# Delta rule's output norm: sums and squares of the next group issued a group ahead, and two of four diagonal matrices built on ScalarE

## The chip, the cores and the metric

The kernel runs on one core of one Trainium2 chip. The metric is the device time of one execution in microseconds, as the median of several runs. The engines named below are TensorE (PE; its weight loads are PEld), VectorE (DVE), ScalarE (ACT), GpSimd (POOL) and SyncE (SP), which issues the loads of weights. Each engine works through its own instructions in the order written and waits on semaphores where the code says so.

## The reference, cut to what matters

The reference is a network of two blocks on 256 tokens of width 1024. The change lies in one step of its second block, the bidirectional gated delta rule with 8 heads of 128 columns. What follows the two scans is:

```
o = jnp.transpose(o_fwd + o_bwd, (0, 2, 1, 3))                          # (B, S, H, 128)
o = o * lax.rsqrt(jnp.mean(o * o, axis=-1, keepdims=True) + RMS_EPS)    # per token and head
o = o * norm_w.astype(f32) * jax.nn.silu(z.astype(f32))
return o.reshape(B, S, H * DV).astype(h.dtype) @ w_out
```

So each row (one token of one head) is divided by its root mean square, multiplied by a gate, and the result goes through the output projection.

## The kernel before

The kernel is hand-written: every engine has a list of instructions fixed by the code, with no scheduler, and counts on semaphores between them. The step around the change is the end of `gdn_solve`. The 8 heads are worked in four groups `q` of two heads; a group has four 128x128 pieces `c` (two heads by two tiles of tokens).

For one group the work passes from engine to engine:

1. PE, `read_out(q)`: 8 pairs of products (16 matmul instructions of 128x128 in the trace, L2535 and L2537) into bank `ps[4 + q]`, then `o_mm`.
2. DVE, L2823: adds `from_state` to that bank, which gives `o` of the group, 128x512, then `o_out`.
3. ACT, L2702: four Square instructions over 128x128, each with a sum over its row into `o_sum` (an activation and a read of the accumulator in the trace), each with `o_square`.
4. DVE, L2825 and L2827: mean plus epsilon, reciprocal, 128x4 each, then `o_means`.
5. ACT, L2705: square root of the four columns into `o_root`, then `o_roots`.
6. DVE, L2835: four diagonal matrices `diag`, identity times a column of `o_root`, then `diag_ready`.
7. PE, L2546, `turn(q)`: four products `o` x `diag` (8 matmul instructions in the trace), which transpose and scale in one, into `ps[q]`, then `o_turned`.
8. DVE, L2809, `gate(q)`; ACT, L2697, `round_out(q)`; DVE, L2816, `split_out(q)`: gate, high part, low part, 128x512 each.

PE's list is `read_out(0)`, `read_out(1)`, `turn(0)`, `read_out(2)`, `turn(1)`, `read_out(3)`, `turn(2)`, the first part of the output projection (8 matmuls, L2558, over the heads of groups 0 and 1), `turn(3)`, and the rest of the output projection. PE's list is the same before and after the change: `read_out(q + 2)` stands behind `turn(q)`.

In the list of DVE, `gate(q - 1)` and `split_out(q - 2)` stand between the reciprocal and the diagonals of group `q`; in ACT's, `round_out(q - 1)` stands behind the root of group `q`. The weights of the output projection are in the ring of four buffers before the step begins, and SP issues nothing during it.

Of the kernel before, what the change touches and what calls it, by code (L numbers as in the profile page):

```python
# [20 lines left out]
ACT = mybir.ActivationFunctionType  # L21
AX = mybir.AxisListType

P = 128
# [153 lines left out]
def carve(k, at, *dims):  # L178

    n = int(np.prod(dims))  # L180
    assert at + n <= k.ARENA, (at, n)
    v = k.arena[:, at:at + n]
    if len(dims) == 1:
        return v
    names = "abcd"[:len(dims)]
    return v.rearrange(f"p ({' '.join(names)}) -> p {' '.join(names)}",
                       **{x: d for x, d in zip(names[1:], dims[1:])})
# [1296 lines left out]
GROUPS = S // GROUP_T  # L1484
# [830 lines left out]
def gdn_solve(k, seam):  # L2315


    g, ps, U, H = k.gdn, k.ps, FIRST, GDN_H
# [10 lines left out]
    lay = Layout(k, g.at_A)  # L2329
    v1, state = lay.take(2 * H, P), lay.take(2 * H, P)  # L2330
    rhs, v2 = g.kq.rearrange("p h (d n) -> p (h d) n", d=2), carve(k, g.at_v, 2 * H, P)
    lay = Layout(k, g.at_kdec + 2 * H * S)
    o, junk, diag = lay.take(2 * H, P), lay.take(4, P), lay.take(2, 4, P)
    gated, from_state = carve(k, g.at_kdec, H, S), carve(k, g.at_kdec, 2 * H, P)
    oT = [k.spare_r[:, n * H * S:(n + 1) * H * S].rearrange("p (h s) -> p h s", h=H) for n in range(2)]
    o_sum, o_mean, o_inv, o_root = (k.small[:, n * 16:(n + 1) * 16] for n in range(4))
# [13 lines left out]
    GROUPS = H // 2  # L2350
# [11 lines left out]
    def group(ap, q):  # L2362
        return ap[:, 4 * q:4 * q + 4, :].rearrange("p c n -> p (c n)")
# [5 lines left out]
    def tensor(pe):  # L2369
# [41 lines left out]
        for h in range(H):  # L2411
            for tt in range(TT):
                c = slice(tt * P, (tt + 1) * P)
                at = (h % 2) * S + tt * P
                last = pe.matmul(ps[h // 2][:, at:at + P], g.kT[:, h, c], g.qT[:, h, c], start=True, stop=True)
# [97 lines left out]
        for q in range(GROUPS):  # L2513


            for c in range(4):
                h, tt = 2 * q + c // 2, c % 2
                last = pe.matmul(ps[4 + q][:, c * P:(c + 1) * P], g.qT[:, h, tt * P:(tt + 1) * P],
                                 state[:, 2 * h + 1 - tt, :], start=True, stop=True)
# [21 lines left out]
        def turn(q):  # L2541


            pe.wait_ge(diag_ready, q + 1)
            for c in range(4):
                last = pe.matmul(ps[q][:, c * P:(c + 1) * P], o[:, 4 * q + c, :], diag[:, q % 2, c, :],  # L2546
                                 start=True, stop=True)
            last.then_inc(o_turned, 1)
# [3 lines left out]
        def out_of(n, tt, parts, heads):  # L2552

            hi, lo = unit_parts(k, U["gdn_out"] + n)
            for m in parts:
                split_ready(k, pe, U["gdn_out"] + n, m)
                for h in heads:
                    last = pe.matmul(out_bank(n, tt), oT[m == 1][:, h, tt * P:(tt + 1) * P], (hi, hi, lo)[m][:, h, :],  # L2558
                                     start=(m == 0 and h == 0), stop=(m == 2 and h == H - 1))
            return last  # L2560

        for q in range(GROUPS):
            read_out(q)
            if q >= 1:
                turn(q - 1)
        pe.wait_ge(o_out, 2)
        pe.wait_ge(o_round, 2)
        for tt in range(TT):
            out_of(0, tt, (0,), range(4))
        turn(3)  # L2570
        pe.wait_ge(o_out, 4)
        pe.wait_ge(o_round, 4)
# [3 lines left out]
        for tt in range(TT):  # L2576
            last = out_of(0, tt, (1, 2), range(H))
        last.then_inc(k.unit_done, 1)
        for n in range(1, 4):
            for tt in range(TT):  # L2580
                last = out_of(n, tt, (0, 1, 2), range(H))
# [4 lines left out]
    def scalar(act):  # L2586
        for h in range(H):
# [6 lines left out]
            for s in range(4):  # L2594
                last = act.activation(g.intraT[:, h, s, :], RI[h % 2][:, s * P:(s + 1) * P], ACT.Exp,
                                      bias=g.negG[:, s, h:h + 1])
# [87 lines left out]
        for q in range(GROUPS):  # L2684
            act.wait_ge(qs_mm, q + 1)
            for c in range(4):
                h, tt = 2 * q + c // 2, c % 2
                last = act.activation(from_state[:, 4 * q + c, :], ps[4 + q][:, c * P:(c + 1) * P], ACT.Copy,
                                      scale=g.eG[:, 2 - tt, h:h + 1])
# [3 lines left out]
        def round_out(q):  # L2693

            act.wait_ge(o_gated, q + 1)
            heads = slice(2 * q, 2 * q + 2)
            act.activation(oT[0][:, heads, :], gated[:, heads, :], ACT.Copy).then_inc(o_round, 1)  # L2697

        for q in range(GROUPS):
            act.wait_ge(o_out, q + 1)  # L2700
            for c in range(4):
                act.activation(junk[:, c, :], o[:, 4 * q + c, :], ACT.Square,  # L2702
                               accum_out=o_sum[:, 4 * q + c:4 * q + c + 1]).then_inc(o_square, 1)
            act.wait_ge(o_means, q + 1)
            act.activation(o_root[:, 4 * q:4 * q + 4], o_inv[:, 4 * q:4 * q + 4], ACT.Sqrt).then_inc(o_roots, 1)  # L2705
            if q >= 1:
                round_out(q - 1)
        round_out(3)
# [7 lines left out]
    def vector(dve):  # L2716
        dve.wait_ge(g.evacuated, H + H // 2)
        for h in range(H):
            dve.wait_ge(keys_mm, h + 1)
            dve.wait_ge(decays_ready, h + 1)  # L2720
            for s in range(4):
                decay = g.dA[:, h % 2, s, :] if s < 2 else g.intraT[:, h, s, :]
                c = slice(s % 2 * P, (s % 2 + 1) * P)
                last = dve.scalar_tensor_tensor(out=g.A[:, h, s, :], in0=decay, scalar=g.beta[:, s, h:h + 1],
                                                in1=KK[h % 2][:, c], op0=ALU.mult, op1=ALU.mult)
# [60 lines left out]
        for h in range(H):  # L2786
            dve.wait_ge(kq_out, h // 2 + 1)
            at = g.intraT[:, h].rearrange("p (d t) n -> p d (t n)", d=2)
# [3 lines left out]
        for q in range(GROUPS):  # L2792

            dve.wait_ge(ks_mm, q + 1)
            for c, (h, d) in enumerate(members[q]):
                s = second_s[d]
                last = dve.scalar_tensor_tensor(out=rhs[:, 2 * h + d, :], in0=ps[q][:, c * P:(c + 1) * P],
                                                scalar=g.nbe[:, s, h:h + 1], in1=g.bv[:, h, s, :],
                                                op0=ALU.mult, op1=ALU.add)
# [5 lines left out]
        def gate(q):  # L2805

            dve.wait_ge(o_turned, q + 1)
            heads = slice(2 * q, 2 * q + 2)
            dve.scalar_tensor_tensor(out=flat(gated[:, heads, :]), in0=ps[q][:, :], scalar=col(k, "gdn_norm"),  # L2809
                                     in1=flat(g.zT[:, heads, :]), op0=ALU.mult, op1=ALU.mult).then_inc(o_gated, 1)  # L2810

        def split_out(q):

            dve.wait_ge(o_round, q + 1)
            heads = slice(2 * q, 2 * q + 2)
            dve.tensor_tensor(oT[1][:, heads, :], gated[:, heads, :], plain(oT[0][:, heads, :]), ALU.subtract)\  # L2816
               .then_inc(o_split, 1)

        for q in range(GROUPS):
            at = slice(4 * q, 4 * q + 4)  # L2820
            dve.wait_ge(o_mm, q + 1)
            dve.wait_ge(qs_out, q + 1)
            dve.tensor_tensor(group(o, q), ps[4 + q][:, :], group(from_state, q), ALU.add).then_inc(o_out, 1)  # L2823
            dve.wait_ge(o_square, 4 * (q + 1))
            own.up(dve.tensor_scalar(o_mean[:, at], o_sum[:, at], 1.0 / P, EPS, ALU.mult, ALU.add))  # L2825
            own.settle(dve)
            dve.reciprocal(o_inv[:, at], o_mean[:, at]).then_inc(o_means, 1)  # L2827
            if q >= 1:
                gate(q - 1)
            if q >= 2:  # L2830
                split_out(q - 2)
            dve.wait_ge(o_out, q + 1)
            dve.wait_ge(o_roots, q + 1)
            for c in range(4):
                last = dve.tensor_scalar(diag[:, q % 2, c, :], k.ident, o_root[:, 4 * q + c:4 * q + c + 1], None,  # L2835
                                         ALU.mult)
                if c < 3:
                    own.up(last)
            last.then_inc(diag_ready, 1)
# [3 lines left out]
        for n in range(4):  # L2843
            dve.wait_ge(k.unit_done, U["gdn_out"] + n + 1)
            for tt in range(TT):
                xs = k.x[:, tt, n * S:(n + 1) * S]
                last = dve.tensor_tensor(xs, xs, ps[(4 + 2 * n + tt) % 8][:, 0:S], ALU.add)
# [5 lines left out]
            if n == 2:  # L2853
                split_lo(k, dve, U["mlp1_0"])
                seam.round_lo(dve, 1)
                seam.round_lo(dve, 2)

    return Stage(gpsimd=gpsimd, tensor=tensor, scalar=scalar, vector=vector)


# [569 lines left out]
def back_half(k, before_experts):  # L3430
# [7 lines left out]
    gdn_layout(k)  # L3438
    project = gdn_project(k, after_experts)
    rule = gdn_solve(k, after_rule)  # L3440
    feed = mlp(k, 0, after_rule, after_feed)
    dilated = ds_layer(k, after_feed, after_dilated)
# [218 lines left out]
```

## Time and profile before

| what | value |
|---|---|
| median of 3 runs | 1942.78 us (1939.44 to 1943.89) |
| profiled execution | 1942.14 us |
| its span | 1940.3 us |
| granted TensorE clock, mean of the span | 0.984 |
| PE busy | 1870.4 us, 96% of the span |
| PEld busy | 1731.5 us, 89% |
| DVE busy | 1293.1 us, 67% |
| ACT busy | 907.9 us, 47% |
| the step of the change, start of the first sum to start of the rest of the projection | 1358.83 to 1378.59 us |

The profiled execution's time is 1.84 us longer than its span, and 0.64 us below the median. Times inside the span are counted from its start. A timeline row gives the start, the time from the start of the first to the end of the last instruction of the row, the engine, the line, what is written from what, and, in brackets, how long the engine stood idle before it and for whom.

### The profile page before, as it was taken

The numbers are of one execution on the slowest core, as the hardware profiler recorded it, in microseconds if no ns is written. First come the engines' busy times: TensorE is split into PE (matmuls) and PEld (weight loads), VectorE is DVE, ScalarE is ACT, GpSimd is POOL, SyncE is SP. The second block draws the span as 40 slices with busy tenths as digits, with TensorE's granted clock in tenths as the row PEclk, the third lists the DMA queues.
The fourth block names the chain that finished last, engine by engine and source line by source line (L and its number), as shares of the span: only waits on it lengthen the run. The fifth ranks groups of instructions, "written<-read, shape, count | busy, mean of one in ns | idle before, by whom it ended". The sixth has DMA issues, their size and how long they took to land. (4 is left out here: it accounts for less than half of the span.)

```text
span 1940.3 us, 31388 instructions
## 1 busy us (share of the span) xinstructions
PE 1870.4 (96%) x13055; PEld 1731.5 (89%) x13055; DVE 1293.1 (67%) x2048; ACT 907.9 (47%) x1206; POOL 18.0 (1%) x24
## 2 busy tenths in 40 slices
PE   7999899999999999999999989978899999999998
PEld 7998898899999999988888879878899889889987
DVE  5667773899788888755555567996566455546654
ACT  6457543343334443444444445775355343445533
POOL 0000000000000000000000000000000001000000
PEclk9999899999999999999999999997999999999999
DMA  6444355354444444465555553320254456625443
GB/s 228 174 159 152 109 177 192 131 176 175 151 151 153 153 153 141 164 227 192 190 191 190 191 197 108 137 83 23 79 182 173 175 214 197 144 70 202 176 171 151
DMA packets 44757, 310.66 MB, mean 160 GB/s; under 512 B 5182, under 2 KB 5694, under 8 KB 8160
## 3 DMA queue, kind: packets, MB, share of 16 engines
q1 hardware_dynamic: 42592, 303.58, 43.4%
q0 software_dynamic: 1472, 4.86, 1.6%
q8 instruction: 87, 1.43, 0.3%
q10 hardware_dynamic: 576, 0.55, 0.1%
q14 instruction: 30, 0.25, 0.0%
HBM read 306.84 MB, written 2.13 MB: 159 GB/s over the span
## 5 line engine op out<-in xcount | busy, mean ns | idle before, releaser
L310 DVE TENSOR_TENSOR s_ring_lo<-s_ring,s_w_hi 128x2048 fp32r<-128x2048 f32 x236 | 540.5, 2291 | 220.9 <-ACT s_w_hi L304 216.3
L304 ACT ACTIVATE s_w_hi<-s_ring 128x2048 fp32r<-128x2048 f32 x235 | 448.4, 1908 | 124.4 <-PE bank L347 53.4
L347 PE MATMUL bank<-s_hT_hi,s_ring_lo 128*128 128x256 f32 x2000 | 282.3, 284 | 8.9 <-DVE s_ring_lo L310 8.7
L347 PE MATMUL bank<-s_hT_hi,s_w_hi 128*128 128x256 f32 x2000 | 288.6, 287 | 2.2 <-ACT s_w_hi L304 1.9
L347 PEld LDWEIGHTS bank<-s_hT_hi,s_ring_lo 128*128 128x128 f32 x2000 | 259.0, 193 | 9.9 <-DVE s_ring_lo L310 9.9
L347 PEld LDWEIGHTS bank<-s_hT_hi,s_w_hi 128*128 128x128 f32 x2000 | 259.1, 193 | 7.0 <-issue 5.6
L1650 PE MATMUL bank<-s_w_hi,s_hT_lo 128*128 128x512 f32 x1008 | 238.8, 389 | 0.3 <-issue 0.3
L1650 PEld LDWEIGHTS bank<-s_w_hi,s_hT_lo 128*128 128x128 f32 x1008 | 189.1, 188 | 39.7 <-issue 0.4
L347 PE MATMUL bank<-s_hT_lo,s_w_hi 128*128 128x256 f32 x1040 | 147.7, 285 | 0.0
L347 PEld LDWEIGHTS bank<-s_hT_lo,s_w_hi 128*128 128x128 f32 x1040 | 136.0, 195 | 0.0
L347 PE MATMUL bank<-s_x_r,s_w_hi 128*128 128x256 f32 x960 | 134.8, 283 | 0.0
L2903 DVE TENSOR_TENSOR s_ring_lo<-s_ring,s_spare_r 128x2048 fp32r<-128x2048 f32 x32 | 73.2, 2291 | 81.6 <-ACT s_spare_r L2889 81.6
L1752 ACT ACTIVATE s_hT_lo<-s_arena 128x512 fp32r (+1 forms) x64 | 40.4, 632 | 184.6 <-PE bank L1650 184.6
L1650 PE MATMUL bank<-s_ring_lo,s_hT_lo 128*128 128x512 f32 x504 | 124.5, 389 | 0.0
L347 PEld LDWEIGHTS bank<-s_x_r,s_w_hi 128*128 128x128 f32 x960 | 123.8, 192 | 0.0
L2930 PE MATMUL bank<-s_spare_r,s_mid_r 128*128 128x512 f32 x512 | 119.5, 389 | 0.0
L2930 PEld LDWEIGHTS bank<-s_spare_r,s_mid_r 128*128 128x128 f32 x512 | 95.9, 188 | 19.8
L1650 PEld LDWEIGHTS bank<-s_ring_lo,s_hT_lo 128*128 128x128 f32 x504 | 94.6, 188 | 19.6
L1929 DVE TENSOR_TENSOR s_hT_lo<-s_arena,s_hT_lo 128x512 fp32r<-128x512 f32 x64 | 44.3, 692 | 90.8 <-ACT s_hT_lo L1752 90.8
L2889 ACT ACTIVATE s_spare_r<-s_ring 128x2048 fp32r<-128x2048 f32 x32 | 61.3, 1917 | 89.4 <-DMA s_ring<-weights 89.3
L1726 ACT ACTIVATE s_arena<-bank 128x344 f32<-128x344 f32 (+31 forms) x64 | 20.5, 320 | 173.7 <-DVE s_arena L1902 173.7
L272 PE MATMUL bank<-s_hT,s_ring 128*128 128x256 f32 x384 | 84.3, 379 | 0.9 <-ACT s_hT L463 0.9
(452 smaller groups left out, 2444.4 us busy)
## 6 DMA issues: line engine op xcount, KB each, us to landing
s_ring<-weights SPq DMA_DIRECT2D x282, 1024.0 KB, 4.8
s_arena<-bias_by_distance POOLq DMA_DIRECT2D x12, 384.0 KB, 7.3
s_arena<-mem SPq DMA_DIRECT2D x1, 1024.0 KB, 6.0
s_x<-x SPq DMA_DIRECT2D x1, 1024.0 KB, 13.9
x_away<-s_x SPq DMA_DIRECT2D x1, 1024.0 KB, 6.3
s_arena<-sub_keys SPq DMA_DIRECT2D x1, 1024.0 KB, 8.4
s_arena<-x_away SPq DMA_DIRECT2D x1, 1024.0 KB, 7.0
out<-s_x SPq DMA_DIRECT2D x2, 512.0 KB, 2.6
```

The costliest lines, as they stand in the source:

```text
L272: last = pe.matmul(out[:, nb * S:(nb + 1) * S], w[:, c, nb * P:(nb + 1) * P], srcT[:, c, :], start=(c == 0), stop=(c == 7))
L304: act.activation(k.w_hi[:, u % 2, :], k.ring[:, u % RING, :], ACT.Copy).then_inc(k.hi_ready, 1)
L310: dve.tensor_tensor(k.ring_lo[:, u % RING, :], k.ring[:, u % RING, :], plain(k.w_hi[:, u % 2, :]), ALU.subtract).then_inc(k.lo_ready, 1)
L347: last = pe.matmul(out[:, nb * S:(nb + 1) * S], w[:, c, nb * P:(nb + 1) * P], h[:, c, :], start=(n == 0 and c == 0), stop=(n == 2 and c == 7))
L1650: last = pe.matmul(ps[4 + 2 * tt + dh][:, :], g[:, b, tt * P:(tt + 1) * P], w[:, b, dh * 512:(dh + 1) * 512], start=(d == 0 and n == 0 and ...
L1726: act.activation(slots_of(k.G, g * GROUP_T)[:, c:, :], bank[g][:, :].rearrange("p (t n) -> p n t", t=GROUP_T)[:, c:, :], ACT.Copy)\
L1752: round_up = lambda d, at: act.activation(weighted_hi[:, d % 2], k.G[:, at, :], ACT.Copy)\
L1929: take = lambda d, at: dve.tensor_tensor(weighted_lo[:, d % 2], k.G[:, at, :], plain(weighted_hi[:, d % 2]), ALU.subtract).then_inc(weight ...
L2889: act.activation(wide_hi[:, u % RING], slot(k, u), ACT.Copy).then_inc(k.hi_ready, 1)
L2903: dve.tensor_tensor(lo, w, plain(wide_hi[:, u % RING]), ALU.subtract).then_inc(k.lo_ready, 1)
L2930: last = pe.matmul(ps[4 + 2 * pair + tt][:, :], m[:, 8 * q + c, tt * P:(tt + 1) * P], w[:, c, at, :], start=(q == 0 and n == 0 and c == 0) ...
```

## The change

Three things change, in ACT's and DVE's lists alone. The add of group `q + 1` is put ahead of the mean of group `q` on DVE. The four squares of group `q + 1` are put ahead of the root of group `q` on ACT (their scratch output has eight pieces where it had four). Of the four diagonals of a group, ACT makes the first two, behind a wait for its own root, and DVE the last two; PE waits for both counts. The diff, whole:

```diff
--- before.py
+++ after.py
@@ -2330,7 +2330,7 @@
     v1, state = lay.take(2 * H, P), lay.take(2 * H, P)
     rhs, v2 = g.kq.rearrange("p h (d n) -> p (h d) n", d=2), carve(k, g.at_v, 2 * H, P)
     lay = Layout(k, g.at_kdec + 2 * H * S)
-    o, junk, diag = lay.take(2 * H, P), lay.take(4, P), lay.take(2, 4, P)
+    o, junk, diag = lay.take(2 * H, P), lay.take(8, P), lay.take(2, 4, P)
     gated, from_state = carve(k, g.at_kdec, H, S), carve(k, g.at_kdec, 2 * H, P)
     oT = [k.spare_r[:, n * H * S:(n + 1) * H * S].rearrange("p (h s) -> p h s", h=H) for n in range(2)]
     o_sum, o_mean, o_inv, o_root = (k.small[:, n * 16:(n + 1) * 16] for n in range(4))
@@ -2541,7 +2541,7 @@
         def turn(q):
 
 
-            pe.wait_ge(diag_ready, q + 1)
+            pe.wait_ge(diag_ready, 2 * (q + 1))
             for c in range(4):
                 last = pe.matmul(ps[q][:, c * P:(c + 1) * P], o[:, 4 * q + c, :], diag[:, q % 2, c, :],
                                  start=True, stop=True)
@@ -2696,13 +2696,24 @@
             heads = slice(2 * q, 2 * q + 2)
             act.activation(oT[0][:, heads, :], gated[:, heads, :], ACT.Copy).then_inc(o_round, 1)
 
-        for q in range(GROUPS):
+        def o_squares(q):
+
             act.wait_ge(o_out, q + 1)
             for c in range(4):
-                act.activation(junk[:, c, :], o[:, 4 * q + c, :], ACT.Square,
+                act.activation(junk[:, 4 * (q % 2) + c, :], o[:, 4 * q + c, :], ACT.Square,
                                accum_out=o_sum[:, 4 * q + c:4 * q + c + 1]).then_inc(o_square, 1)
+
+        o_squares(0)
+        for q in range(GROUPS):
+            if q + 1 < GROUPS:
+                o_squares(q + 1)
             act.wait_ge(o_means, q + 1)
             act.activation(o_root[:, 4 * q:4 * q + 4], o_inv[:, 4 * q:4 * q + 4], ACT.Sqrt).then_inc(o_roots, 1)
+            act.wait_ge(o_roots, q + 1)
+            for c in range(2):
+                last = act.activation(diag[:, q % 2, c, :], k.ident, ACT.Copy,
+                                      scale=o_root[:, 4 * q + c:4 * q + c + 1])
+            last.then_inc(diag_ready, 1)
             if q >= 1:
                 round_out(q - 1)
         round_out(3)
@@ -2816,11 +2827,17 @@
             dve.tensor_tensor(oT[1][:, heads, :], gated[:, heads, :], plain(oT[0][:, heads, :]), ALU.subtract)\
                .then_inc(o_split, 1)
 
-        for q in range(GROUPS):
-            at = slice(4 * q, 4 * q + 4)
+        def add_state(q):
+
             dve.wait_ge(o_mm, q + 1)
             dve.wait_ge(qs_out, q + 1)
             dve.tensor_tensor(group(o, q), ps[4 + q][:, :], group(from_state, q), ALU.add).then_inc(o_out, 1)
+
+        add_state(0)
+        for q in range(GROUPS):
+            at = slice(4 * q, 4 * q + 4)
+            if q + 1 < GROUPS:
+                add_state(q + 1)
             dve.wait_ge(o_square, 4 * (q + 1))
             own.up(dve.tensor_scalar(o_mean[:, at], o_sum[:, at], 1.0 / P, EPS, ALU.mult, ALU.add))
             own.settle(dve)
@@ -2831,7 +2848,7 @@
                 split_out(q - 2)
             dve.wait_ge(o_out, q + 1)
             dve.wait_ge(o_roots, q + 1)
-            for c in range(4):
+            for c in range(2, 4):
                 last = dve.tensor_scalar(diag[:, q % 2, c, :], k.ident, o_root[:, 4 * q + c:4 * q + c + 1], None,
                                          ALU.mult)
                 if c < 3:
```

ACT, from the last copy of `v2` (L2675 in both) to the first rounding, before the change:

```order
L2675 ACTIVATE s_arena<-bank,s_gdn_small 128x128 x2
L2702 ACTIVATE s_arena,s_small<-s_arena 128x128 x4
L2705 ACTIVATE s_small<-s_small 128x4
L2702 ACTIVATE s_arena,s_small<-s_arena 128x128 x4
L2705 ACTIVATE s_small<-s_small 128x4
L2697 ACTIVATE s_spare_r<-s_arena 128x512
```

and after it, where L2703 are the squares, L2711 the root, L2714 the two diagonals and L2697 the rounding:

```order
L2675 ACTIVATE s_arena<-bank,s_gdn_small 128x128 x2
L2703 ACTIVATE s_arena,s_small<-s_arena 128x128 x8
L2711 ACTIVATE s_small<-s_small 128x4
L2714 ACTIVATE s_arena<-s_consts,s_small 128x128 x2
L2703 ACTIVATE s_arena,s_small<-s_arena 128x128 x4
L2711 ACTIVATE s_small<-s_small 128x4
L2714 ACTIVATE s_arena<-s_consts,s_small 128x128 x2
L2697 ACTIVATE s_spare_r<-s_arena 128x512
```

Eight squares, those of groups 0 and 1, now stand ahead of the root of group 0, and the squares of group 2 ahead of the root of group 1.

DVE, from the first add, groups 0 and 1, before the change:

```order
L2823 TENSOR_TENSOR s_arena<-bank,s_arena 128x512
L2825 TENSOR_SCALAR s_small<-s_small 128x4
L2827 RECIPROCAL s_small<-s_small 128x4
L2835 TENSOR_SCALAR s_arena<-s_consts,s_small 128x128 x4
L2823 TENSOR_TENSOR s_arena<-bank,s_arena 128x512
L2825 TENSOR_SCALAR s_small<-s_small 128x4
L2827 RECIPROCAL s_small<-s_small 128x4
L2809 SCALAR_TENSOR_TENSOR s_arena<-bank,s_cols,s_arena 128x512
L2835 TENSOR_SCALAR s_arena<-s_consts,s_small 128x128 x4
```

and after it, where L2834 is the add, L2842 and L2844 mean and reciprocal, L2852 the diagonals and L2820 the gate:

```order
L2834 TENSOR_TENSOR s_arena<-bank,s_arena 128x512 x2
L2842 TENSOR_SCALAR s_small<-s_small 128x4
L2844 RECIPROCAL s_small<-s_small 128x4
L2852 TENSOR_SCALAR s_arena<-s_consts,s_small 128x128 x2
L2834 TENSOR_TENSOR s_arena<-bank,s_arena 128x512
L2842 TENSOR_SCALAR s_small<-s_small 128x4
L2844 RECIPROCAL s_small<-s_small 128x4
L2820 SCALAR_TENSOR_TENSOR s_arena<-bank,s_cols,s_arena 128x512
L2852 TENSOR_SCALAR s_arena<-s_consts,s_small 128x128 x2
```

Two adds, of groups 0 and 1, now stand ahead of the first mean, and two diagonals stand where four stood.

## Rows read from the trace of the kernel before

**Rows 1.** The page, engines: busy us, share of the span, instructions

```profile
PE 1870.4 (96%) x13055; PEld 1731.5 (89%) x13055; DVE 1293.1 (67%) x2048; ACT 907.9 (47%) x1206; POOL 18.0 (1%) x24
```

**Rows 2.** Busy time by stretch: us, engines in turn, clock, DMA share, GB/s

```profile
1358.00:1380.00 22.00, 14.06 (x102) 13.02 (x101) 12.26 (x36) 8.65 (x41) 0.00 (x0) 0.88 0.00 1
...
1400.00:1500.00 100.00, 99.85 (x818) 98.96 (x817) 64.43 (x61) 52.98 (x63) 0.00 (x0) 1.00 0.52 183
```

**Rows 3.** Timeline of PE, through the step

```profile
1356.84 0.39 PE L2535 MATMUL bank<-s_arena 128*128 128x128 f32 x2
...
1360.19 0.39 PE L2537 MATMUL bank<-s_arena 128*128 128x128 f32 x2
1362.53 1.16 PE L2546 MATMUL bank<-s_arena 128*128 128x128 f32 x8 [1.95 <-DVE s_arena L2835]
1363.52 0.39 PE L2535 MATMUL bank<-s_arena 128*128 128x128 f32 x2
...
1365.08 0.39 PE L2537 MATMUL bank<-s_arena 128*128 128x128 f32 x2
1366.27 1.16 PE L2546 MATMUL bank<-s_arena 128*128 128x128 f32 x8 [0.80 <-DVE s_arena L2835]
...
1370.62 1.16 PE L2546 MATMUL bank<-s_arena 128*128 128x128 f32 x8 [1.40 <-DVE s_arena L2835]
...
1374.96 2.08 PE L2546 MATMUL bank<-s_arena 128*128 128x128 f32 x8 [2.24 <-DVE s_arena L2835]
1378.59 3.46 PE L2558 MATMUL bank<-s_w_hi,s_spare_r 128*128 128x256 f32 x16 [1.55 <-issue]
...
1384.76 2.08 PE L2558 MATMUL bank<-s_w_hi,s_spare_r 128*128 128x256 f32 x16
```

**Rows 4.** Timeline of DVE, group 0 and parts of the later ones

```profile
1358.83 0.69 DVE L2823 TENSOR_TENSOR s_arena<-bank,s_arena 128x512 f32<-128x512 f32 x1 [5.19 <-PE bank L2537]
1360.87 0.17 DVE L2825 TENSOR_SCALAR s_small<-s_small 128x4 f32<-128x4 f32 x1 [1.34 <-ACT s_arena L2702]
1361.07 0.18 DVE L2827 RECIPROCAL s_small<-s_small 128x4 f32<-128x4 f32 x1
1361.60 0.87 DVE L2835 TENSOR_SCALAR s_arena<-s_consts,s_small 128x128 f32<-128x128 f32 x4 [0.34 <-ACT s_small L2705]
1362.38 0.68 DVE L2823 TENSOR_TENSOR s_arena<-bank,s_arena 128x512 f32<-128x512 f32 x1
...
1368.46 0.72 DVE L2809 SCALAR_TENSOR_TENSOR s_arena<-bank,s_cols,s_arena 128x512 f32<-128x512 f32 x1
1369.10 0.68 DVE L2816 TENSOR_TENSOR s_spare_r<-s_arena,s_spare_r 128x512 fp32r<-128x512 f32 x1
1369.69 0.87 DVE L2835 TENSOR_SCALAR s_arena<-s_consts,s_small 128x128 f32<-128x128 f32 x4
...
1377.08 0.75 DVE L2809 SCALAR_TENSOR_TENSOR s_arena<-bank,s_cols,s_arena 128x512 f32<-128x512 f32 x1 [2.17 <-PE bank L2546]
```

**Rows 5.** Timeline of ACT in the step

```profile
1359.56 0.31 ACT L2702 ACTIVATE s_arena<-s_arena 128x128 f32<-128x128 f32 x1 [1.36 <-DVE s_arena L2823]
1359.77 0.19 ACT L2702 ACTIVATION_READ_ACCUMULATOR s_arena<-s_arena 128x1 f32 x1
...
1361.29 0.20 ACT L2705 ACTIVATE s_small<-s_small 128x4 f32<-128x4 f32 x1 [0.45 <-DVE s_small L2827]
...
1377.86 0.63 ACT L2697 ACTIVATE s_spare_r<-s_arena 128x512 fp32r<-128x512 f32 x1 [3.67 <-DVE s_arena L2809]
```

**Rows 6.** The same timeline earlier: sixteen scaled 128x128 copies out of PSUM

```profile
1350.79 4.24 ACT L2688 ACTIVATE s_arena<-bank,s_gdn_small 128x128 f32<-128x128 f32 x16 [2.36 <-PE bank L2518]
```

**Rows 7.** PE by stretch: us, busy (instructions), granted clock, DMA share, GB/s

```profile
1370.60:1374.90 4.30, 2.11 (x16) 0.98 0.00 0
1374.90:1378.50 3.60, 2.08 (x8) 0.50 0.00 0
1378.50:1381.50 3.00, 2.91 (x13) 0.50 0.00 0
```

## The prediction

> **What bounds the kernel now.** I read the page first: PE is busy 96% of the span, DVE 67%, ACT 47% [rows 1]. Then the busy time by stretch: around the change it looks different. In 1358 to 1380 us PE is busy 14.06 of 22 us, DVE 12.26, ACT 8.65, with no DMA at work; in 1400 to 1500 us PE is busy 99.85 of 100 [rows 2]. So this step is bound by a chain between engines, nothing is loaded in it, and PE is full behind it: what the step loses or gains goes into the time one for one. Last, the timelines of the three engines, to follow the chain. PE's four `turn`s start at 1362.53, 1366.27, 1370.62 and 1374.96 us, each after an idle time that DVE's diagonals end, and the rest of the projection starts at 1378.59 [rows 3]. The intervals are 3.74, 4.35, 4.34 and 3.63 us.
>
> What a group takes, from group 0: the add starts at 1358.83, the squares at 1359.56 (0.73 later), the mean at 1360.87 (1.31), the root at 1361.29 (0.42), the diagonals at 1361.60 (0.31), `turn` at 1362.53 (0.93) [rows 3 to 5]. The next add starts at 1362.38, right behind the diagonals, though PE had ended `read_out(1)` at 1360.19 + 0.39 = 1360.58. That wait looks like something to save. The point of this prediction is what the look-ahead hangs on instead.
>
> **The change, step by step.** The squares of group q + 1 now stand ahead of the root of group q. They need the add of q + 1, which needs `read_out(q + 1)`. On PE, `read_out(q + 2)` stands behind `turn(q)`. So the new chain is: `turn(q)`, `read_out(q + 2)`, add, four squares, and only then the root of q + 1, its diagonals and `turn(q + 1)`. Before, `read_out(q + 2)` had the whole of DVE's and ACT's work on group q + 1 to hide behind; now it is on the path. Behind ACT's waiting square stand the root, the two diagonals and the rounding; for the root wait DVE's diagonals and PE.
>
> Root to `turn`. Before it is 1362.53 - 1361.29 = 1.24 us. Now DVE makes two diagonals: 0.31 to its first, 0.20 between two (four take 0.87 and one takes 0.28: (0.87 - 0.28) / 3), 0.28 for the last, 0.05 to PE: 0.84. ACT's half: no row shows ACT waiting for its own result. Nearest are the root's 0.20 us and DVE's reciprocal, which starts 0.20 after the mean that it needs [rows 4, 5]; 0.20 to 0.31 bounds it. A scaled copy from SBUF isn't shown either: a square of that size takes 0.31 and lets the next start after 0.21 [rows 5], and sixteen scaled copies out of PSUM take 4.24, 0.265 each [rows 6]. So 0.20 to 0.31, plus 0.21 to 0.265, plus 0.31, plus 0.05: 0.77 to 0.94. I take 0.84 for both halves, as DVE's and the middle of ACT's agree: 0.4 us saved a group, the bounds of ACT's half adding up to 0.1 each. The Trainium skill ("VectorE: DVE Perf Modes", section on the TRN2 errata) says that ScalarE pays a fixed extra on each SBUF-source instruction, exposed between instructions. This trace agrees in the duration of one (0.31 us for a square), but not in the spacing, since the next starts after 0.21 [rows 5]; by the page two copies would take 0.1 us more than by the row, in each of four groups.
>
> Group 0. `read_out(1)` ends at 1360.58, the add of group 1 starts at 1360.60, its squares 0.73 later at 1361.33. They hold ACT for 1.19 us (the 1.31 above less the signal and the 0.10 by which the next instruction starts before the last one has ended), so the root of group 0 starts at 1362.52, where it started at 1361.29. The mean and reciprocal (0.42) are hidden in that. `turn(0)` starts at 1362.52 + 0.84 = 1363.36: 0.83 later than before.
>
> Groups 1 and 2. From `turn(q)`: 0.99 to the start of `read_out(q + 2)` (1362.53 to 1363.52), 1.95 to its end (1365.08 + 0.39) [rows 3], 0.02 to the add, 0.73 to the squares, 1.19 to the root, 0.84 to the next `turn`: 5.72 us. DVE's work of the interval fits: add 0.59 to the next, mean 0.20, reciprocal 0.10, gate 0.64, split 0.59 [rows 4], 2.12 us against the 2.23 from the add to its diagonals. `turn(1)` starts at 1369.08 and `turn(2)` at 1374.80, which were 1366.27 and 1370.62.
>
> Group 3. No more look-ahead, and mean and reciprocal are early. But the gate of group 2 stands ahead of the diagonals of group 3 on DVE and waits for `turn(2)`: 1.16 for it, 0.04 to the gate, 0.64 gate, 0.59 split [rows 3, 4], 0.20 + 0.28 + 0.05 for the diagonals: 2.96 where it was 4.34. `turn(3)` starts at 1377.76, was 1374.96.
>
> The rest, `turn(3)` to the projection, stays: 2.08 and 0.04, the gate 0.78, the rounding 0.73 [rows 3 to 5]. In all +2.8 us (0.83 + 1.98 + 1.37 - 1.38), with TensorE's clock as it is now.
>
> **The clock.** In 1370.6 to 1374.9 PE was busy 2.11 of 4.30 us, and the granted clock fell to 0.50, that is 1.2 in place of 2.4 GHz, through `turn(3)` and to 1381.5 [rows 7]. `turn(3)` took 2.08 where the others took 1.16, and 16 matmuls of the projection 3.46 where such a row at full clock takes 2.08 [rows 3]: before already pays 0.92 + 1.38 = 2.3 us. After the change PE is idle 5.72 - 2.94 = 2.8 us before each `turn`, more than the 2.24 us of idle time around which it fell. `turn` and `read_out` at the lower level are 2.94 x 2.08 / 1.16 = 5.3 us: 2.3 more for each such interval. Nothing at all extra, or even the 2.3 given back if the clock happens to be full at the end, is the one bound: +2.8 - 2.3 = +0.5. Both intervals and `turn(2)` low is the other: 2.8 + 4.6 + 0.9 = +8.3. I take one interval low: the idle time is longer than where it fell, but between there are 2.9 busy us. The Trainium skill ("TensorE: Matmul & The Clock Gate", what's actually happening) says that the clock follows how busy PE has been recently; the fall in the rows agrees, and by this rule the change, which lengthens PE's idle times, tends to lose more than its chain does.
>
> **The sum.** Against the profiled execution, 1942.14 us (1940.3 of span and 1.84 around it; 0.64 below the median): 1942.14 + 2.8 + 2.3 = 1947.2 us. That is 4.4 us or 0.23% above the median. I count 0.2%, 3.9 us, as about what a measurement of this kernel can tell from no change.
>
> **The rivals.**
> - *The chain alone.* The clock falls no more than before, or gives something back: +0.5 to +3.8, around 1944.9, which can't be told from no change. For it speaks that `turn` and `read_out` fill half of each interval; against it that the clock fell with 2.11 of 4.30 us busy. 0.30.
> - *The clock low in most of the step:* +6.5 to +8.3, around 1949.4. For it: three idle times of 2.8 us in a row. Against it: with the clock low PE is busy for more of the time, and at 1381.5 it came back after 2.91 busy us of 3.00 [rows 7]. 0.13.
> - *The look-ahead works, faster.* If the add and squares of group q + 1 were done when the root of q is due, squares and sum would be off the path, and intervals would shrink to PE's own 2.94 us: (3.74 + 4.35 + 4.34) - 3 x 2.94 = 3.6, plus 0.4 in group 0, so 1938.1. It is decided by whether `read_out(q + 1)` ends 1.9 us (0.73 + 1.19) before the root of q is due. In group 0 it ends at 1360.58 and the root is due at 1361.29, 0.7 us: too late by 1.2; later it stands behind the `turn` of the group before last. Only if ACT could take its root ahead of a waiting square could this be; its rows stand in the order written. The Trainium skill ("TensorE: Matmul & The Clock Gate", architectural detail) calls ScalarE's queue strictly first in, first out, with which these rows agree. 0.04.
> - *The change cancels out:* the 0.4 saved in each group meets a look-ahead less late than worked out, within 1.5 us of zero, 1942 to 1943. 0.05.
>
> The likeliest case, the chain and about one interval's clock (+3.8 to +6.5, 1945.9 to 1948.6), has 0.48. Of it about 0.09 lies below the bound. So slower by over 0.2%: 0.39 + 0.13 = 0.52; within: 0.30 + 0.09 + 0.05 = 0.44; faster: 0.04. For 8 in 10 the range takes in most of the chain alone (from +1.9) and of the low clock (to +7.9): 1944.0 to 1950.0.
>
> **What would show it.** In the changed kernel's timeline: the first root 1.2 us later after the first add than before (3.7 in place of 2.46); `turn` intervals of 5.7, 5.7 and 3.0; ACT's squares idle for DVE's add ahead of each root; two diagonals on each engine, `turn` 0.84 behind the root; PE's idle time 2.8 ahead of `turn(0)` to `turn(2)`; the granted clock below 1.00 somewhere in 1361 to 1378. Wrong would be: intervals under 4.4 us (the chain isn't through `read_out`), a clock at full all through the step (the chain alone), or a last `turn` less than 2 us later than before.

## The result, and the profile after

The changed kernel takes 1947.89 us (median of 14 runs, 1943.17 to 1949.78), where the kernel before takes 1941.49 us (median of 14, 1938.84 to 1944.9). The ratio is 1.003, with a 95% interval of 1.0022 to 1.0037: slower by 0.2 to 0.4%, beyond the 0.2% that the prediction set. The forecast was 1947.2 us, with a range of 1944.0 to 1950.0.

The profiled execution has a span of 1945.6 us, 5.3 more than before. PE's timeline through the step, beside [rows 3] (L2546 is `turn`, L2535 and L2537 `read_out`, L2558 the projection):

```profile
1358.59 0.39 PE L2537 MATMUL bank<-s_arena 128*128 128x128 f32 x2
1361.89 1.16 PE L2546 MATMUL bank<-s_arena 128*128 128x128 f32 x8 [2.91 <-ACT s_arena L2714]
1362.89 0.41 PE L2535 MATMUL bank<-s_arena 128*128 128x128 f32 x2
...
1365.66 0.63 PE L2537 MATMUL bank<-s_arena 128*128 128x128 f32 x2
1369.21 1.43 PE L2546 MATMUL bank<-s_arena 128*128 128x128 f32 x8 [2.92 <-ACT s_arena L2714]
...
1376.69 2.03 PE L2546 MATMUL bank<-s_arena 128*128 128x128 f32 x8 [2.91 <-ACT s_arena L2714]
...
1380.56 1.16 PE L2546 MATMUL bank<-s_arena 128*128 128x128 f32 x8 [0.18 <-DVE s_arena L2852]
1383.27 3.47 PE L2558 MATMUL bank<-s_w_hi,s_spare_r 128*128 128x256 f32 x16 [1.55 <-issue]
```

Three times PE stands idle for 2.9 us until ScalarE's diagonals come. The intervals between turns are 7.32, 7.48 and 3.87 us, where they were 3.74, 4.35 and 4.34. A last row of `read_out` (1365.66 here) lasts 0.63, where it took 0.39 at full clock: the clock is low there. DVE's timeline, beside [rows 4] (L2834 is the add, L2852 two diagonals):

```profile
1357.23 0.69 DVE L2834 TENSOR_TENSOR s_arena<-bank,s_arena 128x512 f32<-128x512 f32 x1 [5.19 <-PE bank L2537]
...
1366.33 0.69 DVE L2834 TENSOR_TENSOR s_arena<-bank,s_arena 128x512 f32<-128x512 f32 x1 [4.62 <-PE bank L2537]
...
1373.82 0.69 DVE L2834 TENSOR_TENSOR s_arena<-bank,s_arena 128x512 f32<-128x512 f32 x1 [4.80 <-PE bank L2537]
```

and ACT's, beside [rows 5] (L2703 the squares, L2711 the root, L2714 the two copies that make diagonals):

```profile
1367.05 0.31 ACT L2703 ACTIVATE s_arena<-s_arena 128x128 f32<-128x128 f32 x1 [5.21 <-DVE s_arena L2834]
...
1368.24 0.19 ACT L2711 ACTIVATE s_small<-s_small 128x4 f32<-128x4 f32 x1
1368.46 0.69 ACT L2714 ACTIVATE s_arena<-s_consts,s_small 128x128 f32<-128x128 f32 x2
```

DVE waits 4.6 and 4.8 us for `read_out`, ACT 5.2 us for DVE, and the root of group 1 comes at 1368.24, right behind the squares of group 2. Its mean and reciprocal had been ready before. The clock by stretch (us, PE busy, granted clock, DMA share, GB/s), beside [rows 7]:

```profile
1361.80:1369.20 7.40, 4.40 (x24) 0.77 0.01 2
1369.20:1376.60 7.40, 4.57 (x24) 0.77 0.00 0
1376.60:1380.50 3.90, 3.69 (x16) 0.56 0.00 0
1380.50:1383.20 2.70, 1.16 (x8) 1.00 0.00 0
1383.20:1386.20 3.00, 2.93 (x15) 0.57 0.00 0
```

A granted clock of 0.50 is the lower level (1.2 GHz), 1.00 the full one (2.4 GHz), and a value between them is a mean over time at each: it switches between the two all through the step. I measure a step's length from the first add to the start of the projection. It was 1378.59 - 1358.83 = 19.76 us and is 1383.27 - 1357.23 = 26.04: 6.3 longer. The span grew by less because in this execution all that lies ahead of the first add was 1.6 us shorter, and what lies behind 0.6 longer.

### The profile page after: what moved, and what is told of

It reads as the page before. It is cut to its first block and busy times, and to the rows that moved or that the text cites. A ratio compares the mean times of both kernels' runs of the same rounds, so it can differ in the third digit from the quotient of the medians.

```text
span 1945.6 us, 31388 instructions
## 1 busy us (share of the span) xinstructions
PE 1873.2 (96%) x13055; PEld 1734.3 (89%) x13055; DVE 1292.0 (66%) x2040; ACT 909.5 (47%) x1214; POOL 18.0 (1%) x24
```

## The experiments

The theory: the look-ahead made the root of group q + 1 wait for `read_out(q + 2)`, which stands behind `turn(q)` on PE, so that each `turn` waits for a `read_out` behind the one before it; and PE's longer idle times let its clock fall. The rivals were ScalarE's share of the diagonals as the cause, and the squares' place in ScalarE's list by itself. All ratios are to the kernel before, run beside each of them, with 95% intervals: its median was 1942.48 us beside e1 to e4, 1942.53 beside e5 to e8 and 1943.06 beside e9 and e10, so the ratios tell more than the medians. Step lengths are as above, of one profiled execution each.

| kernel | median us | ratio | step us | turn intervals us |
|---|---|---|---|---|
| before | 1941.49 | 1 | 19.76 | 3.74, 4.35, 4.34 |
| changed | 1947.89 | 1.003 (1.0022 to 1.0037) | 26.04 | 7.32, 7.48, 3.87 |
| e1 diagonals only | 1942.75 | 0.9994 (0.9983 to 1.0005) | 17.27 | 3.22, 3.96, 3.95 |
| e2 look-ahead only | 1950.4 | 1.0045 (1.0032 to 1.0058) | 26.97 | 6.12, 8.66, 3.63 |
| e3 changed, PE's order | 1939.09 | 0.9983 (0.9974 to 0.9992) | 16.23 | 2.78, 3.07, 3.00 |
| e4 before, PE's order | 1942.47 | 1.0002 (0.9993 to 1.0011) | 18.85 | 3.74, 4.35, 4.35 |
| e5 changed, PE kept busy | 1944.29 | 1.0009 (1.0 to 1.0018) | 22.09 | 5.87, 5.85, 3.00 |
| e6 before, PE kept busy | 1940.95 | 0.9992 (0.9983 to 1.0001) | 18.83 | 3.74, 4.34, 4.35 |
| e7 changed, late squares | 1945.85 | 1.0015 (1.0006 to 1.0024) | 22.72 | 5.05, 7.27, 3.91 |
| e8 late squares, PE's order | 1936.79 | 0.997 (0.9958 to 0.9982) | 15.93 | 2.78, 2.98, 3.37 |
| e9 diagonals, PE's order | 1941.3 | 0.9994 (0.9984 to 1.0004) | 17.27 | 3.22, 3.96, 3.95 |
| e10 e8, PE kept busy | 1938.56 | 0.9977 (0.9968 to 0.9986) | 15.25 | 2.79, 2.98, 2.99 |

The instructions ahead of the first add are the same in all twelve kernels, yet their traces reach it between 1354.83 us (e5) and 1360.10 (e2). So from one trace each the steps can be compared, and whole times only to some 5 us. The profiled executions of e5 and e10 are the fastest of their 11 runs, 4.8 and 5.1 us below the medians.

**e1, the diagonals alone** (edit of the kernel before):

```diff
-            pe.wait_ge(diag_ready, q + 1)
+            pe.wait_ge(diag_ready, 2 * (q + 1))
...
             act.activation(o_root[:, 4 * q:4 * q + 4], o_inv[:, 4 * q:4 * q + 4], ACT.Sqrt).then_inc(o_roots, 1)
+            act.wait_ge(o_roots, q + 1)
+            for c in range(2):
+                last = act.activation(diag[:, q % 2, c, :], k.ident, ACT.Copy,
+                                      scale=o_root[:, 4 * q + c:4 * q + c + 1])
+            last.then_inc(diag_ready, 1)
...
-            for c in range(4):
+            for c in range(2, 4):
```

> The kernel before with one part of the change: two of the four diagonals of a group on ScalarE, no look-ahead. The theory (the look-ahead carries the loss, the split of the diagonals is a small gain): root to turn about 1.0 us in place of 1.24 in group 0, intervals between turns 3.3, 4.0 and 4.0 in place of 3.74, 4.35 and 4.34, the time 1 to 4 us below the kernel before (the chain 1.3, the rest if the clock then falls less). The rival (the scaled copies on ScalarE and its wait for its own root are what costs): intervals longer than before, 2 us or more slower.

The intervals came as expected and the step is 2.5 us shorter, so ScalarE's copies don't lose anything in it: 0.3 us up to the first `turn`, 1.3 in the intervals, and 0.9 because `turn(3)` now ran at full clock. Yet the time isn't measurably lower, where 1 to 4 us had been expected. In its profiled execution what lies behind the step, from the start of the projection to the end of the span, is 1941.0 - 1374.59 = 566.4 us, against 1940.3 - 1378.59 = 561.7 before. Where that went, in stretches of e1 (us, PE busy, clock, DMA share, GB/s):

```profile
1374.50:1381.50 7.00, 6.91 (x36) 0.58 0.00 0
...
1640.00:1648.00 8.00, 8.00 (x40) 0.59 0.57 105
```

and of the same places before:

```profile
1378.50:1385.50 7.00, 6.91 (x47) 0.78 0.00 0
1638.80:1650.80 12.00, 11.15 (x73) 1.00 0.65 139
```

In the first 7 us of the projection the clock is lower (36 matmuls done in place of 47), and 260 us later, in the dilated attention, it falls where it didn't before. These two, (0.78 - 0.58) x 7 = 1.4 us and (1.00 - 0.59) x 8 = 3.3 us of full clock, are the 4.7 us. That is one execution of e1; its 12 runs lie between 1936.2 and 1946.01, and whether the later fall is in most of them isn't known. It doesn't explain the ratio either: e9 below has the same step length and the same ratio, and its trace is at 1.00 through that piece.

**e2, the look-ahead alone** (the changed kernel, `diag` by DVE for `c in range(4)` again, no copies on ACT, PE waits for `q + 1`).

> The changed kernel with all four diagonals back on VectorE, the look-ahead alone. The theory: the chain turn, read_out, add, squares, root is in it whole, intervals 6.1 us at full clock and up to 7.6 at the low one, the time 5 to 9 us above the kernel before, at least as slow as the changed kernel. The rival (ScalarE's diagonals carry the loss): at the time of the kernel before, within 2 us.

As the theory had it in the main: the step is the longest, 7.2 us over before, and the first interval 6.12. The second, with the clock low, is 8.66, more than the 7.6 expected. The look-ahead carries the whole loss. In the step the split of the diagonals makes up 0.9 us of it; in the time the intervals of the two ratios overlap, so that isn't shown. The rival that ScalarE's diagonals cost is out.

**e3 and e4, PE's order** (the changed kernel, and the kernel before):

```diff
         for q in range(GROUPS):
             read_out(q)
-            if q >= 1:
-                turn(q - 1)
+            if q >= 2:
+                turn(q - 2)
+        turn(2)
```

> The changed kernel with one more edit: TensorE takes read_out(q + 2) ahead of turn(q) in place of behind it. The theory (the look-ahead fails because read_out of its group stands behind a turn that it holds up): squares wait for nothing of PE any more, intervals 2.8 to 3.1 us in place of 7.3, 7.5 and 3.9, the clock not fallen or fallen once, the time 3 to 6 us below the kernel before. The rival (squares ahead of the root are bad for ScalarE's own load, whatever PE does): intervals over 4.4 us, no faster than before.

> The kernel before with TensorE's new order alone (read_out(q + 2) ahead of turn(q)), no look-ahead and all diagonals on VectorE. A control for the run before it: by the theory the turns start when they did, intervals 3.7, 4.35 and 4.35, and the chain gives nothing; the clock may move the time by -2 to +1 us. The rival (TensorE's order is a gain by itself): 3 us or more faster with shorter intervals.

PE's timeline in e3:

```profile
1362.64 1.16 PE L2546 MATMUL bank<-s_arena 128*128 128x128 f32 x8 [1.13 <-ACT s_arena L2715]
1365.42 1.06 PE L2546 MATMUL bank<-s_arena 128*128 128x128 f32 x8
1368.49 1.16 PE L2546 MATMUL bank<-s_arena 128*128 128x128 f32 x8 [2.02 <-ACT s_arena L2715]
```

With the same lists on ACT and DVE as in the changed kernel, and only `read_out` moved ahead, the step falls from 26.04 to 16.23 us and the kernel is 0.17% faster than before, 1.0030 against 0.9983. The same order in the kernel before gives nothing in the time (1.0002) or the intervals between turns. Its step is 0.9 us shorter, by the clock. It was low around `turn(2)` in e4, where PE then had to wait for DVE all the same, and no longer in `turn(3)`, where the projection waits for it:

```profile
1371.08 1.63 PE L2546 MATMUL bank<-s_arena 128*128 128x128 f32 x8 [3.19 <-DVE s_arena L2836]
1375.43 1.16 PE L2546 MATMUL bank<-s_arena 128*128 128x128 f32 x8 [1.01 <-DVE s_arena L2836]
```

So the cause of the longer chain is the pair: a look-ahead, and a producer (`read_out(q + 2)`) that stands on PE behind `turn(q)`. The squares' place alone isn't it.

**e5 and e6, PE kept busy.** Products whose results are overwritten, on PE alone:

```diff
+        def fill(bank, n):
+            for i in range(n):
+                pe.matmul(ps[bank][:, 0:P], g.qT[:, 0, 0:P], g.qT[:, 1, 0:P], start=True, stop=True)
...
             if q >= 1:
+                fill(q - 1, [10, 10, 10][q - 1])
                 turn(q - 1)
```

In e6 the counts are 0, 0 and 4, and `fill(3, 7)` stands ahead of `turn(3)`.

> The changed kernel with work added on TensorE that only keeps it busy: ten products of 128x128 (twenty matmul instructions, about 2.2 us at full clock) ahead of each of turn(0), turn(1) and turn(2), where it stood idle for 2.9 us. Their results are overwritten. The theory (beside the longer chain the clock's fall costs 2 to 3 us): granted clock at 1.00 from the first add to turn(2), intervals near 5.8, 5.8 and 3.0 in place of 7.3, 7.5 and 3.9, the time 2 to 5 us below the changed kernel, so 0 to 4 us above the kernel before. The rival (the clock's level doesn't matter here, the chain alone is longer than was worked out): time within 1 us of the changed kernel or above it.

> The kernel before with such busy work: four products ahead of turn(2) and seven ahead of turn(3), inside its idle times of 1.4 and 2.2 us. The theory: intervals unchanged at 3.74, 4.35 and 4.34, turn(3) at 1.16 us in place of 2.08 and the projection's first sixteen matmuls nearer 2.1 than 3.5, the time 0 to 3 us below the kernel before. The rival (the fall has nothing to do with this idle time): the same clock and time as before.

The clock by stretch in e5 (us, PE busy, clock, DMA share, GB/s):

```profile
1355.00:1377.00 22.00, 17.52 (x148) 1.00 0.00 1
1377.00:1384.00 7.00, 7.00 (x59) 1.00 0.16 21
```

and in e6:

```profile
1359.60:1378.40 18.80, 13.39 (x110) 1.00 0.00 1
1378.40:1385.40 7.00, 6.95 (x58) 1.00 0.10 18
```

and PE's timeline in e5:

```profile
1359.49 1.16 PE L2546 MATMUL bank<-s_arena 128*128 128x128 f32 x8 [0.68 <-ACT s_arena L2722]
1365.36 1.16 PE L2546 MATMUL bank<-s_arena 128*128 128x128 f32 x8 [0.68 <-ACT s_arena L2722]
1371.21 1.16 PE L2546 MATMUL bank<-s_arena 128*128 128x128 f32 x8 [0.68 <-ACT s_arena L2722]
...
1374.21 1.16 PE L2546 MATMUL bank<-s_arena 128*128 128x128 f32 x8 [0.88 <-DVE s_arena L2860]
1376.92 2.15 PE L2558 MATMUL bank<-s_w_hi,s_spare_r 128*128 128x256 f32 x16 [1.55 <-issue]
```

Both run at full clock, and this parts the two terms. In e5 PE still waits 0.68 us for ScalarE's diagonals behind the added products, so these aren't on the chain themselves. Chain: 22.09 - 18.83 = 3.3 us. Clock: 26.04 - 22.09 = 3.9 us in the changed kernel, 19.76 - 18.83 = 0.9 before, a difference of 3.0. Together they are the 6.3. Each is from one trace. In the times e5 gives back about 0.2% of the changed kernel's 0.3%; for e6 the interval reaches just past 1.

**e7, late squares** (the changed kernel):

```diff
         for q in range(GROUPS):
-            if q + 1 < GROUPS:
-                o_squares(q + 1)
             act.wait_ge(o_means, q + 1)
...
             last.then_inc(diag_ready, 1)
+            if q + 1 < GROUPS:
+                o_squares(q + 1)
             if q >= 1:
                 round_out(q - 1)
```

> The changed kernel with the squares of group q + 1 moved behind the root and diagonals of group q on ScalarE, the look-ahead of the add on VectorE kept. It parts the squares' share of the loss from the add's. The theory: the first root is again 0.4 us behind its mean, but mean still stands behind the add of the next group, which waits for read_out: turns start about 0.1 us later than before in group 0, then intervals of 5.0, 5.6 and 3.0, the stage 1 to 2 us longer than before and 2 us shorter than in the changed kernel, the time 0 to 4 us above the kernel before. The rival (the squares ahead of the root were the only bad step): no slower than e1, 1 to 4 us below the kernel before.

```profile
1363.22 1.16 PE L2546 MATMUL bank<-s_arena 128*128 128x128 f32 x8 [2.03 <-ACT s_arena L2712]
1368.27 1.95 PE L2546 MATMUL bank<-s_arena 128*128 128x128 f32 x8 [2.10 <-DVE s_arena L2852]
1375.54 2.08 PE L2546 MATMUL bank<-s_arena 128*128 128x128 f32 x8 [2.70 <-DVE s_arena L2852]
```

The first interval, at full clock, is 5.05 as worked out. The second, with the clock low, is 7.27, not 5.6, and the step 3.0 us over before, not 1 to 2: I had left the clock out of that number. About half the loss in time is gone (1.0015 for 1.003), so squares ahead of the root are one part of it; the add ahead of the mean on DVE, which waits for `read_out` as well, is the other. The rival that the squares were the only bad step is out.

**e8 and e9, what the look-ahead is worth.** e8 is e7 with PE's order of e3; e9 is e1 with it.

> The same with TensorE taking read_out(q + 2) ahead of turn(q). The theory: no wait for read_out is left in a look-ahead, intervals 2.8 to 3.1, the first turn 0.9 us earlier than in e3; the stage 1 us shorter than e3's, the time 3 to 7 us below the kernel before. The rival (squares behind the diagonals now wait on ScalarE's list and hold the next root): intervals over 3.5 us, no better than e3.

> The kernel before with two diagonals on ScalarE and TensorE taking read_out(q + 2) ahead of turn(q), no look-ahead. It tells what the look-ahead is worth once TensorE's order suits it, beside e8. The theory: intervals as in e1 (3.2, 4.0 and 4.0), since squares are still on the path of every group, the stage 1.5 us longer than e8's, the time 1 to 4 us below the kernel before and 1 to 4 us above e8. The rival (with TensorE's order right, the look-ahead adds nothing): stage and time of e8.

e8 is 0.3% faster than the kernel before (0.997), the lowest ratio here, from 6 runs; its interval overlaps e3's. Its step is only 0.3 us shorter than e3's, not 1 us. It starts its first turn 0.9 us earlier after the first add (3.78 against 4.67), but the clock fell around `turn(2)` and took part of that back. e9 has e1's intervals and step, which are 1.3 us longer than e8's, and a time that can't be told from before. The intervals of e8's and e9's ratios don't meet (0.9982 and 0.9984 are their nearest ends). So the look-ahead is a gain once its producer stands ahead.

**e10, e8 with PE kept busy** (`fill` of six ahead of `turn(2)`, three ahead of `turn(3)`, five behind it).

> e8 with busy work on TensorE inside the idle times left: six products ahead of turn(2), three ahead of turn(3) and five behind it. The theory: clock at 1.00 through the step, intervals 2.8, 3.0 and 3.0 and the start of the projection at full clock, the stage 0 to 1 us and the time 0 to 2 us below e8. The rival (busy work delays the turns or buys nothing): time at e8's or above it.

```profile
1364.89 1.16 PE L2546 MATMUL bank<-s_arena 128*128 128x128 f32 x8 [0.59 <-DVE s_arena L2862]
...
1367.88 1.16 PE L2546 MATMUL bank<-s_arena 128*128 128x128 f32 x8
1370.59 2.15 PE L2558 MATMUL bank<-s_w_hi,s_spare_r 128*128 128x256 f32 x16 [0.43 <-issue]
```

The step is 15.25 us, the shortest, all at full clock. The time isn't below e8's: 0.9977 against 0.997, intervals that overlap widely. The expected gain isn't shown, and where it went isn't settled. The two traces don't tell: e10's span is 4.0 us shorter than e8's, but 3.6 of this lie ahead of the first add.

## Why the prediction was right

**What bounds the step**: right. PE waits for diagonals three times and is full behind the step; 6.3 us more in the step stand beside 6.4 us more between the medians. That they agree so closely is partly luck, as the time ahead of the first add alone differs by up to 5 us between traces. So is the distance of only 0.7 us between forecast and result: the rise was 6.4 us where 4.4 above the median of that time had been forecast, and that median, of 3 runs, was 1.3 us higher than the one of 14 runs.

**The chain through `read_out`**: right, by its rows (DVE waiting 4.6 and 4.8 us for it, ACT 5.2 for DVE) and by e2, e3 and e7. The prediction asked for a first root 3.7 us behind the first add: it is 1360.93 - 1357.23 = 3.70. The `turn` came 0.96 behind it, not 0.84.

**Root to `turn`** is the term that was mis-sized. The chain has it in this order, of the changed kernel:

```profile
1368.33 0.10 ACT s_small L2711
1368.44 0.02 issue
1368.46 0.70 ACT s_arena L2714 x2
1369.16 0.04 issue
1369.21 1.43 PE bank L2546 x8
```

ScalarE's wait for its own root is 0.22 us from start to start (taken: 0.20 to 0.31), but its two copies take 0.70, where 0.21 + 0.31 = 0.52 was the low bound and 0.265 + 0.31 = 0.58 the high. All eight copies of the changed kernel (ns: shortest, median, longest):

```profile
L2714 ACT ACTIVATE s_arena<-s_consts,s_small x8: 385/394/402, 1361.1 to 1377.6; 128x128 f32<-128x128 f32 x8
```

A scaled copy takes 0.39 us, not a square's 0.31, and the second starts 0.69 - 0.39 = 0.30 behind the first. So ScalarE's half, not DVE's, ends last. The low bound rested on a misread row: what starts 0.21 behind the square at 1359.56 [rows 5] is the read of its accumulator. The next square of the kernel before starts 0.31 behind it:

```profile
1359.87 0.29 ACT L2702 ACTIVATE s_arena<-s_arena 128x128 f32<-128x128 f32 x1
```

The Trainium skill ("VectorE: DVE Perf Modes", section on the TRN2 errata) says that ScalarE's extra for an SBUF source is exposed between instructions, once for each small tile. The copies' spacing of 0.30, more than the 0.265 out of PSUM, agrees, so its reading, which the prediction set 0.1 us a group above the row's, was the nearer one. The squares can't tell, as a read of the accumulator stands between each two. The difference of 0.13 comes into three turns and is most of what the chain is longer than worked out, 3.3 for 2.8 us: e5's intervals at full clock are 5.87 and 5.85, not 5.72, and the last is 3.00, not 2.96.

**The clock**: the right direction and nearly the size. The prediction took 2.3 us (one interval low) over the chain; e5 and e6 give 3.0. It wasn't one interval low and one full, but each of the two partly, at 0.77, and `turn(2)` at 0.56, which held up the gate of group 2: that is the last interval's 3.87 for 2.96. The Trainium skill ("TensorE: Matmul & The Clock Gate", what's actually happening) says that the clock follows how busy PE has been recently. In the step the traces agree: with products added in PE's idle times e5 and e6 ran at 1.00. Elsewhere busy time as the profile counts it isn't the whole of it: in 1326 to 1340 us of the kernel before, mostly through matmuls of 32x32 and 64x64, PE was busy 13.98 of 14.00 us with the clock at 0.50.

**The sum**: the step came out 6.3 us longer where 5.1 had been worked out, 0.5 of the miss from the chain and 0.7 from the clock. The chain alone (+0.5 to +3.8) and the cancelling case are out. Between the likeliest case (up to +6.5) and the clock low in most of the step (from +6.5) the result doesn't decide: the step's +6.3 lies at the bound, and the ratio's interval, +4.3 to +7.2 us, takes in part of both. The look-ahead as a gain was a rival with the condition that `read_out` ends early enough; e3 and e8 make that condition true, and then the gain comes (0.9983 and 0.997), about the 4.0 us reckoned there: 0.17% or 3.3 us in e3, 0.3% or 5.8 in e8, with intervals that take in 4.0 in both. In e3's step three terms make up the 3.5 us: the intervals between turns 3.6 shorter, as reckoned, the first `turn` 1.0 later, where 0.4 earlier had been reckoned, and 0.9 of clock given back in `turn(3)`.

## What to carry to other kernels

Before work is put a group ahead on one engine, follow its producer through every other engine's list: if the producer stands behind something that the delayed work releases, the look-ahead turns a hidden step into a link of the chain. Then move the producer ahead as well (here PE's `read_out`, which had banks of its own), and put the early work behind the urgent one in each list. Where TensorE waits in a short step, count the clock too, and try a gain at its full length: a step 2.5 us shorter (e1) gave no time back that could be measured.

## What the runs showed of the hardware

TensorE's clock was worth about as much as the chain in this step: 3.9 of the changed kernel's 26.04 us, shown by adding work that does nothing. A low clock cost time in the step only where something waited for PE: around `turn(2)` it was low in e4 (1.63 us for 1.16) and e9 (2.07), and their steps were as long as e6's and e1's, which were at full clock there (18.85 and 18.83, twice 17.27). Where the clock falls differs between traces: in e1's profiled execution it fell at 1640 us, through a piece that had run at full clock before, and cost 3.3 us. That the shorter step brought this about isn't shown, as e9, with a step of the same length, had no such fall. On ScalarE a 128x128 copy from SBUF with a scale per partition takes 0.39 us and lets the next start after 0.30, where a square of the same size with a sum takes 0.29 to 0.31, its accumulator read starts 0.20 to 0.22 behind it, and the next square 0.29 to 0.31 behind it.
